# A routed expert's output phase for 96 tokens: from one block of 96 rows to four lanes of 32 rows

## The chip, the cores and the metric

The kernel runs on one core of a Trainium2 chip, in one launch, and all its data is f32. The metric is the device time of that core in microseconds, the median of several runs. Times inside the program come from one profiled execution. A tensor multiplication of f32 stands in the trace as two rows (two weight loads and two matmuls), one for each of its two passes over the same columns.

## The reference, cut to what matters

Two layers are computed for 128 context tokens and 256 latent tokens of width 1024. The change touches only the last part, a SwiGLU with eight experts of which each token uses two:

```
def moe_swiglu(h, w_router, wg, wu, wd):
    t = h.reshape(-1, shp[-1])                     # all 384 tokens
    logits = einsum('td,de->te', t, w_router)
    top_logit, top_e = lax.top_k(logits, 2)
    gates = softmax(top_logit, axis=-1)
    ...                                            # tokens sorted by expert
    def expert_block(args):
        xb, e = args
        return (silu(xb @ wg[e]) * (xb @ wu[e])) @ wd[e]
    ...
    y = zeros_like(t).at[tok_sorted].add(out[dest] * gate_sorted[:, None])
```

`wg` and `wu` are 8 x 1024 x 2816, `wd` is 8 x 2816 x 1024. The 384 tokens give 768 pairs of token and expert.

## The kernel before

Tokens lie on partitions, 128 to a tile, D = 1024 columns. After the attention layer's part the router's result is put into a table (`vtab`) that names a width for each expert: 64, 96, 128, 160, 192, 256 or 384 tokens. `PIECES` splits a width into pieces of 64, 96 or 128 tokens. For the inputs here the experts run as 128+64, 96, 96, 128, 96+64, 96, 64 and 64 tokens (experts 0 to 7), so four pieces have 96 tokens: experts 1, 2 and 5, and the first piece of expert 4.

TensorE has a copy of an expert's code for each of the eight experts and seven widths, and `go_to` branches to the right one by compares (L1044) at the end of the expert before.

An expert's weights come in 33 loads of 1 MB (`MOE_CHUNKS`), issued by SyncE (`moe_load`, L2055) into 11 slots. SyncE issues load n when `moe_used` has reached n - 10, and TensorE raises `moe_used` as it is done with a slot. The last slot of an expert isn't counted (`owed[0] = 0` in `expert`), so 256 increments stand against 264 loads.

An expert has three parts on TensorE:
- **hidden** (L894): for five groups of four 128-wide tiles of the hidden dimension (f tiles 0 to 19), gate and up, tokens as the stationary operand and 512 weight columns moving, over eight k-steps. A piece of 96 tokens is already laid in four lanes of 32 rows of the result: three lanes hold the three token groups of 32 for columns 0 to 383, the fourth holds columns 384 to 511 for each group in turn, side by side. ScalarE does SiLU, VectorE multiplies, and `turn_act` transposes (L939, L943 for 96 tokens).
- **hidden_rest** (L919): the last two f tiles, gate and up in one bank, for 96 tokens as one block of 96 rows and 256 columns. `turn_rest` (L965) transposes them, in the middle of the output part.
- **output** (L992): for 22 f tiles the transposed activations are stationary (128 x tokens) and 512 of the 1024 columns of `wd` move, into two banks. Eleven loads of two f tiles each.

ScalarE and VectorE copy the two banks to `yt`, GpSimd writes them to `expert_out` in DRAM by indirect DMA, one whole-row write for each of the three possible pieces (`y_rows`), and one of half rows (`y_halves`) for the first two, which serves pieces of 64 tokens: `YWRITES = 5` an expert. Row numbers out of bounds are skipped. After expert 7 GpSimd waits for all writes, gathers the rows of each token's later expert, and VectorE adds them to X.

TensorE carries out its own list in order. What else can delay it is a weight load that hasn't landed, or a bank not yet emptied.

## Time and profile before

| | us |
|---|---|
| median of three runs | 2201.76 |
| lowest, highest | 2199.25, 2204.59 |
| the profiled execution | 2182.95 |
| its span, first to last instruction | 2181.0 |
| PE (matmul) busy | 1990.3 |
| PE, weight loads busy | 1282.2 |
| VectorE, ScalarE, GpSimd busy | 445.1, 385.0, 126.8 |
| mean granted TensorE clock | 0.955 of full |

PE busy is the time in which a matmul is under way, several of them counted once. The eight experts take the time from 1190 to 2157 us, 44% of the span; ahead of them are the first layer, attention and the router.

### The profile page before, as it was taken

To read this page: it belongs to the slowest core of one execution; us is meant where nothing else is said; L and a number is where in the kernel's file an instruction comes from. 1 tells how busy PE (TensorE), PEld (TensorE's weight loads), DVE (VectorE), ACT (ScalarE), POOL (GpSimd) and SP (SyncE) were. 2 spreads that over 40 slices of the span, in tenths; PEclk is the share of its full clock that TensorE was granted. 3 is DMA by queue.
4 is the path that set the end of the run, shared out by engine and by line. 5 is a ranking of instruction groups with operands and counts; after the bars stand their busy time and mean duration, and the time that the engine had idled before them with its cause. 6 is when DMAs were issued, how large, how long until landed. Compare 5 with 4: busy or idle time off the path is not lost.

```text
span 2181.0 us, 26973 instructions
## 1 busy us (share of the span) xinstructions
PE 1990.3 (91%) x11623; PEld 1282.2 (59%) x11623; DVE 445.1 (20%) x1078; ACT 385.0 (18%) x819; POOL 126.8 (6%) x104
## 2 busy tenths in 40 slices
PE   4999987799999999987986999999999999998764
PEld 2554547786555578744585554868545774764341
DVE  2440126311000000146423010111011110111032
ACT  2221211302000000243311110212121110122220
POOL 0000123200000000000001000101010100101011
PEclk8999997899999999998897999999999999999998
DMA  9564411022644551221053555899988665899996
GB/s 332 199 228 154 154 60 37 1 78 84 211 168 158 185 163 54 95 69 40 1 178 120 193 193 196 294 342 330 330 282 299 232 215 198 289 335 348 372 386 238
DMA packets 232516, 427.65 MB, mean 196 GB/s; under 512 B 16030, under 2 KB 87165, under 8 KB 232062
## 3 DMA queue, kind: packets, MB, share of 16 engines
q1 hardware_dynamic: 219086, 412.49, 54.1%
q0 software_dynamic: 10208, 12.09, 1.6%
q8 instruction: 111, 1.82, 0.3%
q10 hardware_dynamic: 3088, 1.06, 0.2%
q14 instruction: 23, 0.19, 0.0%
HBM read 427.52 MB, written 25.85 MB: 208 GB/s over the span
## 4 chain that ended last, share of the span: by engine, by line
PE 68%; DMA 7%; DVE 4%; issue 2%; ACT 1%; POOL 0%; SPq 0%; DVEq 0%; POOLq 0%; ACTq 0%
PE bank L894 21%; PE bank L992 13%; PE bank L676 11%; PE bank L497 7%; PE bank L694 5%; PE bank L919 2%; DMA ring<-in_moe_w_gate_dram 2%; DMA ring<-in_moe_w_down_dram 2%; PE bank L435 2%; DMA ring<-in_moe_w_up_dram 1%; PE bank L467 1%; PE bank L766 1%; DMA arena<-in_moe_w_gate_dram 1%; PE bank L765 1%; PE bank L741 1%
## 5 line engine op out<-in xcount | busy, mean ns | idle before, releaser
L894 PE MATMUL bank<-ring,HTXN 128*32 128x128 f32 (+3 forms) x4352 | 410.7, 396 | 45.9 <-issue 18.2
L894 PEld LDWEIGHTS bank<-ring,HTXN 128*32 128x32 f32 (+2 forms) x4352 | 292.6, 122 | 157.0 <-issue 115.5
L1066 ACT ACTIVATE arena<-bank 128x512 f32<-128x512 f32 (+2 forms) x328 | 152.2, 529 | 555.2 <-PE bank L992 197.7
L992 PE MATMUL bank<-ring,arena 128*64 128x512 f32 (+2 forms) x640 | 230.8, 599 | 8.3 <-DMA ring<-in_moe_w_down_dram 8.3
L676 PE MATMUL bank<-HTXN,ring 128*128 128x384 f32 x704 | 231.7, 490 | 2.7 <-DVE HTXN L1412 2.7
L497 PE MATMUL bank<-ring,HTXN 128*128 128x512 f32 (+4 forms) x624 | 196.6, 476 | 3.7 <-DVE HTXN L1412 2.7
L676 PEld LDWEIGHTS bank<-HTXN,ring 128*128 128x128 f32 x704 | 133.6, 191 | 94.8 <-issue 5.5
L1836 DVE TENSOR_TENSOR arena<-arena,bank 128x512 f32<-128x512 f32 x120 | 76.6, 682 | 503.6 <-PE bank L894 503.6
L992 PEld LDWEIGHTS bank<-ring,arena 128*64 128x64 f32 (+2 forms) x640 | 79.6, 157 | 142.7 <-issue 122.0
L497 PEld LDWEIGHTS bank<-ring,HTXN 128*128 128x128 f32 x624 | 114.6, 191 | 81.6 <-issue 71.6
L1340 ACT ACTIVATE arena<-bank 128x512 f32<-128x512 f32 x120 | 65.0, 599 | 404.1 <-PE bank L894 397.3
L694 PE MATMUL bank<-ring,arena 128*128 128x256 f32 x528 | 114.2, 379 | 0.0
L694 PEld LDWEIGHTS bank<-ring,arena 128*128 128x128 f32 x528 | 100.2, 190 | 13.6
L894 PE MATMUL bank<-arena,HTXN 128*32 128x384 f32 (+3 forms) x1088 | 103.6, 393 | 4.3 <-DMA arena<-in_moe_w_up_dram 2.4
L894 PEld LDWEIGHTS bank<-arena,HTXN 128*32 128x32 f32 (+2 forms) x1088 | 72.4, 121 | 31.0 <-issue 19.4
L992 PE MATMUL bank<-arena 128*64 128x512 f32 (+2 forms) x240 | 86.5, 599 | 4.0 <-DMA arena<-in_moe_w_down_dram 4.0
L518 PE MATMUL bank<-HTXN,ring 128*128 128x384 f32 x256 | 83.5, 487 | 1.8 <-DVE HTXN L1412 1.8
L497 PE MATMUL bank<-ring,arena 128*128 128x256 f32 x384 | 83.1, 379 | 1.5 <-DVE arena L1620 1.5
L497 PEld LDWEIGHTS bank<-ring,arena 128*128 128x128 f32 x384 | 72.9, 190 | 11.6 <-issue 1.7
L467 PE MATMUL bank<-ring,sv 128*2 128x512 f32 x384 | 51.0, 653 | 20.6 <-DMA ring<-in_w_mod_dram 20.6
L518 PEld LDWEIGHTS bank<-HTXN,ring 128*128 128x128 f32 x256 | 48.3, 190 | 34.9 <-issue 2.0
L435 PE MATMUL bank<-CST,arena 128*128 128x128 f32 x252 | 42.4, 315 | 26.3 <-DVE arena L1681 14.5
(269 smaller groups left out, 1473.8 us busy)
## 6 DMA issues: line engine op xcount, KB each, us to landing
ring<-in_moe_w_gate_dram SPq DMA_DIRECT2D x64, 1024.0 KB, 6.5
ring<-in_moe_w_up_dram SPq DMA_DIRECT2D x64, 1024.0 KB, 6.6
ring<-in_moe_w_down_dram SPq DMA_DIRECT2D x64, 1024.0 KB, 7.1
ring<-in_w_mod_dram SPq DMA_DIRECT2D x24, 2048.0 KB, 12.2
arena<-in_moe_w_gate_dram SPq DMA_DIRECT2D x24, 1024.0 KB, 7.8
arena<-in_moe_w_up_dram SPq DMA_DIRECT2D x24, 1024.0 KB, 8.2
arena<-in_moe_w_down_dram SPq DMA_DIRECT2D x24, 1024.0 KB, 6.7
ring<-in_w_in_dram SPq DMA_DIRECT2D x10, 2048.0 KB, 9.1
```

What stands on the lines that cost most here:

```text
L435: last = tp(bank[:, k * P:(k + 1) * P], src, ident)
L467: last = mm(bank[q:q + 2, :], sv[:, :, k], w[:, k, :], start=(k < 4), stop=(k >= 4))
L497: last = mm(bank[:, 0:width], lhs[:, k, t * P:(t + 1) * P], w[:, k, :], start=(k == 0), stop=(k == kt - 1))
L518: last = mm(bank[:, 0:TOK], w[:, k, m * P:(m + 1) * P], HT[:, k, :], start=(k == 0), stop=(k == KT - 1))
L676: last = mm(bank[:, 0:TOK], w[:, k, m * P:(m + 1) * P], HT[:, k, :], start=(k == 0), stop=(k == KT - 1))
L694: last = mm(banks[t][0][:, 0:256], aT[:, FH * fh + f, t * P:(t + 1) * P], w[:, f, :], start=(fh == 0 and f == 0), stop=(fh == 1 and f == F ...
L894: last = mm(bank[row:row + rows_, col:col + cn], xe[:, i, k, at:at + rows_], wt[:, c0:c0 + cn], start=(k == 0 and col == 0), stop=(k == KT ...
L919: last = mm(bank[lane * w:(lane + 1) * w, at:at + width], xe[:, i, k, 0:w], wt[:, k, lane * width:(lane + 1) * width], start=(k == 0), sto ...
L992: last = mm(out, act_of(f, i, w), wt[:, f % 2, 512 * h:512 * h + 512], start=(f == 0), stop=(f == FT - 1))
L1066: return act_fn(out, in_, ACT.Copy)
L1340: act_fn(sgm[:, j % 2, i, :], moe_bank_of(("g", j, i))[:, :], ACT.Silu).then_inc(moe_drained(("g", j, i), e)[0], 1)
L1836: v.tensor_tensor(a, a, moe_bank_of(("u", j, i))[:, :], ALU.mult).then_inc(moe_drained(("u", j, i), e)[0], 1)
```

## The change

The output part of a 96-token piece gets the form that the hidden part has. Lanes 0 to 2 (32 tokens each) hold output columns 0 to 767: 512 in the first bank, 256 in the second. The fourth lane holds columns 768 to 1023 of the three token groups in turn, two in the first bank and one in the second. `hidden_rest` is laid out likewise (three lanes of 192 columns and 3 x 64 in the fourth, for gate and for up), and `turn_rest` gathers from it.

In `yt` the last quarter of the rows of tokens 0 to 95 then stands in rows 96 to 127. GpSimd writes the whole rows first (with a last quarter that means nothing), waits for that write to land (`y_whole`), and then issues three writes of quarter rows (`y_quarters`, `write_corner`), which put the right values in place. They are issued for every expert; for a first piece that isn't of 96 tokens their rows are out of bounds. The order of the pieces' writes is reversed. VectorE computes the rows of the corner writes once, in front of the experts.

```diff
-YWRITES = 5
+YWRITES = 7
...
+            v.tensor_scalar(is96, vsum, 1.0, None, ALU.is_equal)
+            for n in range(3):
+                v.tensor_scalar(corner_no[:, 8 * n:8 * n + 8], cnt, lane_row[n], NOROW, ALU.is_le, ALU.mult)
+                last = v.tensor_scalar(corner_f[:, 8 * n:8 * n + 8], base, lane_row[n], 4.0, ALU.add, ALU.mult)
...
+            v.tensor_copy(corner_i, corner_f)
...
                     w = pieces[i][1]
-                    width = 128 * halves(w)
+                    if w == 64:
+                        parts = [(64 * n, 0, 0, 64, 128 * n, 128) for n in range(2)]
+                    elif w == 96:
+                        parts = ([(32 * n, 0, 32 * n, 32, 0, 192) for n in range(3)]
+                                 + [(96, 64 * n, 32 * n, 32, 192, 64) for n in range(3)])
+                    else:
+                        parts = [(0, 0, 0, P, 0, 256)]
...
+                        if w == 96:
+                            tp(bank[:, at:at + w], sgm[0:w, HC % 2, i, 0:P], ident[0:w, 0:w])
+                            tp(bank[0:64, at + w:at + 2 * w], sgm[0:w, HC % 2, i, P:P + 64], ident[0:w, 0:w])
+                            for m in range(3):
+                                last = mm(bank[64:P, at + w + 32 * m:at + w + 32 * m + 32], sgm[w:P, HC % 2, i, 64 * m:64 * m + 64], ident[w:P, w:P],
+                                          start=True, stop=True)
+                            continue
...
+            OUT_96 = ([(0, 32 * n, 0, n, 0, 512) for n in range(3)] + [(0, 96, 0, 0, 768, 256), (0, 96, 256, 1, 768, 256)]
+                      + [(1, 32 * n, 0, n, 512, 256) for n in range(3)] + [(1, 96, 0, 2, 768, 256)])
+
+            def output_96(bank0, bank1, a, wt, f):
+
+                for b, row, col, group, c0, cn in OUT_96:
+                    bank, full = (bank0, bank1)[b]
+                    last = mm(bank[row:row + 32, col:col + cn], a[:, 32 * group:32 * group + 32], wt[:, c0:c0 + cn],
+                              start=(f == 0 and col == 0), stop=(f == FT - 1 and (b == 1 or row < 96 or col > 0)))
+                    if f == 0 and (b, row) == (0, 0):
+                        settle(last)
+                    if f == FT - 1 and row == 96 and (b == 1 or col > 0):
+                        last.then_inc(full, 1)
+                return last
...
+                            if w == 96:
+                                last = output_96(banks[i, 0], banks[i, 1], act_of(f, i, w), wt[:, f % 2, :], f)
+                                continue
...
+                whole = g_.indirect_dma_start(y_rows, at_row(30 + 8 * i + e), yt[:, i, :], None, bounds_check=ROWS - 1, oob_is_err=False)
+                whole.then_inc(y_whole if i == 0 else y_written, 16)
...
+            def write_corner(e, n):
+                g_.indirect_dma_start(y_quarters, at_row(88 + 8 * n + e), yt[:, 0, 256 * n:256 * n + 256], None,
+                                      bounds_check=4 * ROWS - 1, oob_is_err=False).then_inc(y_written, 16)
...
-                for i in range(NPIECE):
+                for i in reversed(range(NPIECE)):
                     write_out(e, i)
+                pool.wait_ge(y_whole, 16 * (e + 1))
+                for n in range(3):
+                    write_corner(e, n)
```

TensorE in the code of a 96-token expert, from `hidden_rest` to the branches at its end, before (rows that repeat are counted behind an x, one for each matmul; the size is weight columns or rows by moving columns):

```order
L919 MATMUL bank<-arena,HTXN 96x256 x16
L939 MATMUL bank<-CST,arena 128x96 x3
L943 MATMUL bank<-CST,arena 128x32 x3
L992 MATMUL bank<-ring,arena 96x512 x8
L965 MATMUL bank<-CST,arena 128x96 x2
L992 MATMUL bank<-ring,arena 96x512 x8
L867 MATMUL bank<-CST,HTXN 128x128 x8
L992 MATMUL bank<-ring,arena 96x512 x16
L992 MATMUL bank<-arena 96x512 x12
L1044 COMPARE_AND_BRANCH x6
```

The same place now, one k-step of `hidden_rest` (there are 16), the turn of it, one f tile of the output part, and the branches:

```order
L932 MATMUL bank<-arena,HTXN 32x192 x3
L932 MATMUL bank<-arena,HTXN 32x64 x3
...
L977 MATMUL bank<-CST,arena 128x96
L978 MATMUL bank<-CST,arena 64x96
L980 MATMUL bank<-CST,arena 64x32 x3
...
L994 MATMUL bank<-arena 32x512 x3
L994 MATMUL bank<-arena 32x256 x6
L1081 COMPARE_AND_BRANCH x6
```

A tile f of the output part was two matmuls of 96 rows and is nine of 32 rows; a k-step of `hidden_rest` for one of gate and up was one and is six.

GpSimd at an expert's end, before:

```order
L1940 DMA expert_out<-arena,idx 768x1024
L1943 DMA expert_out<-arena,idx 1536x512
L1940 DMA expert_out<-arena,idx 768x1024
L1943 DMA expert_out<-arena,idx 1536x512
L1940 DMA expert_out<-arena,idx 768x1024
```

and now, where only the last five stand behind the drain of piece 0:

```order
L1989 DMA expert_out<-arena,idx 768x1024 x2
L1992 DMA expert_out<-arena,idx 1536x512
L1989 DMA expert_out<-arena,idx 768x1024
L1992 DMA expert_out<-arena,idx 1536x512
L1996 DMA expert_out<-arena,idx 3072x256 x3
```

The writes of pieces 2 and 1 went ahead of those of piece 0, and three corner writes came behind.

## Rows read from the trace of the kernel before

**Rows 1.** Stretches: experts 1, 2, 4, 5, 6; busy time, instructions, clock, DMA share.

```profile
core 0: us, PE busy (x) PEld busy (x) DVE busy (x) ACT busy (x) POOL busy (x), PEclk, DMA share, GB/s
...
1375.42:1479.19 103.77, 102.68 (x1121) 75.24 (x1120) 14.26 (x24) 20.29 (x41) 7.96 (x8) 1.00 0.94 333
1479.19:1582.89 103.70, 102.61 (x1122) 75.45 (x1122) 14.27 (x24) 20.29 (x41) 7.96 (x8) 1.00 0.95 332
...
1700.94:1869.50 168.56, 167.69 (x1613) 108.30 (x1612) 14.89 (x24) 21.25 (x41) 7.96 (x8) 1.00 0.60 207
1869.50:1973.28 103.78, 102.69 (x1122) 75.25 (x1121) 14.26 (x24) 20.29 (x41) 7.96 (x8) 1.00 0.94 328
1973.28:2058.13 84.85, 66.36 (x492) 34.22 (x491) 14.86 (x25) 19.70 (x40) 6.98 (x7) 1.00 1.02 376
```

**Rows 2.** Expert 1: L919's min/median/max ns and starts; then in order of time.

```profile
L919 PE MATMUL bank<-arena,HTXN x32: 379/379/457, 1432.6 to 1439.4; 128*96 128x256 f32 x32
...
1439.92 0.37 PE L943 MATMUL bank<-CST,arena 32*128 32x32 f32 x3
1440.21 7.11 PE L992 MATMUL bank<-ring,arena 128*96 128x512 f32 x16
1447.16 0.33 PE L965 MATMUL bank<-CST,arena 96*128 96x96 f32 x2
...
1468.80 10.46 PE L992 MATMUL bank<-arena 128*96 128x512 f32 x24
```

**Rows 3.** 1415.90 to 1426.50, hidden part: the stretch, then groups (busy, mean ns).

```profile
1415.90:1426.50 10.60, 10.60 (x194) 10.42 (x192) 1.88 (x3) 2.46 (x6) 0.00 (x0) 1.00 1.04 402
...
L894 PE MATMUL bank<-ring,HTXN 128*32 128x128 f32 x96 | 10.7, 273 | 0.0
L894 PE MATMUL bank<-ring,HTXN 128*32 128x384 f32 x96 | 10.5, 487 | 0.0
L943 PE MATMUL bank<-CST,arena 32*128 32x32 f32 x2 | 0.3, 222 | 0.0
```

**Rows 4.** Branches ending experts 1, 2, 4, 5, 6: ns min/median/max, starts.

```profile
L1044 PEldq COMPARE_BRANCH  x2: 63/2215/4367, 1471.4 to 1471.5; - x2
...
L1044 PEldq COMPARE_BRANCH  x1: 4618/4618/4618, 1575.2 to 1575.2; - x1
...
L1044 PEldq COMPARE_BRANCH  x2: 75/1706/3337, 1864.0 to 1864.2; - x2
...
L1044 PEldq COMPARE_BRANCH  x3: 63/63/4220, 1965.5 to 1965.7; - x3
...
L1044 PEldq COMPARE_BRANCH  x3: 63/75/6242, 2056.2 to 2056.5; - x3
```

**Rows 5.** Matmuls from expert 1's first compare (1471.40) to 1479.19: busy, mean ns.

```profile
L992 PE MATMUL bank<-arena 128*96 128x512 f32 x19 | 8.3, 592 | 0.0
```

**Rows 6.** Expert 2, hidden part: the sequencer's wait, and its group in time.

```profile
L891 PEldq EVENT_SEMAPHORE  x1: 51/51/51, 1495.8 to 1495.8; - x1
...
1497.05 5.45 PE L894 MATMUL bank<-ring,HTXN 128*32 128x384 f32 x96
```

**Rows 7.** PE in order of time, from expert 6 to expert 7.

```profile
2056.19 1.94 PE L992 MATMUL bank<-arena 128*64 128x512 f32 x8 [0.62 <-DMA arena<-in_moe_w_down_dram]
2062.98 9.23 PE L894 MATMUL bank<-ring,HTXN 128*64 128x256 f32 x64 [4.85 <-issue]
```

**Rows 8.** Stretches behind expert 6's last matmul (columns as in rows 1).

```profile
2058.80:2062.90 4.10, 0.00 (x0) 0.00 (x0) 0.00 (x0) 0.00 (x0) 2.35 (x3) 0.70 1.05 387
2062.90:2066.00 3.10, 3.02 (x15) 1.91 (x17) 0.00 (x0) 0.00 (x0) 2.49 (x3) 0.50 0.83 295
2066.00:2070.00 4.00, 4.00 (x34) 2.77 (x32) 0.00 (x0) 0.62 (x2) 0.08 (x1) 0.84 0.58 170
```

**Rows 9.** Order of time: DVE as expert 0 begins; GpSimd after the last drain.

```profile
1206.07 0.69 DVE L1836 TENSOR_TENSOR arena<-arena,bank 128x512 f32<-128x512 f32 x1 [22.70 <-PE bank L894]
...
2158.84 1.02 POOL L1940 DMA_INDIRECT expert_out<-arena,idx  x1 [79.75 <-ACT arena L1066]
```

35 lines of the change are left out of this document (23 added, 12 removed).

## The prediction

> **What bounds the kernel now.** I read first the stretches of the single experts, then the order of time of TensorE in one 96-token expert, then the branches between experts, and last the two experts at the end. The experts run from 1190 to 2157 of the 2181 us. TensorE is busy in all but 1 us of an expert with a 96-token piece: 102.7 of 103.8 us [rows 1]. There are four such pieces: experts 1, 2 and 5 hold one each (103.8, 103.7 and 103.8 us), expert 4 holds one beside a 64-token piece (168.6 us). In these the time is TensorE's, so matmul time saved there should arrive at the end. Experts 6 and 7 hold 64 tokens each and wait for weights: PE is busy 66.4 of 84.9 us while the DMA engines are full, share 1.02 [rows 1]. The change leaves these two as they are; their transfers are tied to the matmuls ahead of them, so they move forward with the end of expert 5.
>
> In expert 1 the output phase runs from 1440.21 to 1479.19, 39.0 us [rows 2]. A matmul of f32 shows as two rows, one for each pass over its columns.
>
> **Output phase, the gain.** 24 passes of 512 columns with 96-column weights take 10.46 us in all, one of them 0.592 [rows 2, 5]: (10.46 - 0.59)/23 = 0.429 us from one to the next. A tile f has four, 1.716 us. A pass of 256 columns is (1439.4 - 1432.6)/31 = 0.219 us from the next [rows 2]. In the new form lanes 0 to 2 have per f two passes of 512 and two of 256, 2 x (0.429 + 0.219) = 1.30 us; the fourth lane has six of 256, 1.31 us. This holds only if the four lanes run beside each other. The hidden phase of the same piece already has this shape: 96 passes of 384 columns and 96 of 128 in 10.60 us, each kind busy for all of it, so 32 rounds of 0.331 us, in which three lanes do 384 columns and the fourth three times 128 [rows 3]. I take 1.30 us. Saved: 22 x (1.716 - 1.30) = 9.2 us for a piece.
>
> **The last hidden tile pair (L919).** Now 32 passes of 256 columns, 32 x 0.219 = 7.0 us [rows 2]. New: 16 k-steps of two rounds, in a round three lanes of 192 columns and in the fourth three passes of 64. By columns a pass of 64 is 0.056 us (0.110, 0.219 and 0.429 for 128, 256 and 512 lie on 0.83 ns a column and 3 ns), a round 0.168, together 5.4 us. The trace has no round so short. The nearest small passes are the transposes of 32 columns, (0.37 - 0.22)/2 = 0.07 us apart [rows 2, 3]: three are 0.21 a round, 6.7 us. If a round can't be shorter than the 0.331 seen with the same number of instructions [rows 3], it is 10.6 us, a loss of 3.6. I take 5.6, near the columns' value since the lanes of [rows 3] are at it exactly: 1.4 saved, ends +1.6 and -3.6.
>
> **The turn of that pair (L965)** was two transposes, 0.33 us [rows 2]; two remain and three small matmuls of two passes come, 6 x 0.07 = 0.4 us, with a change of array shape: +0.5.
>
> Together 9.2 + 1.4 - 0.5 = 10.1 us a piece, **40.4 us** for four.
>
> **What it loses: the cover of the branches.** At the end of each expert TensorE's instruction stream compares and branches to the next expert's code, and the branch that is taken lasts 3.3 to 6.2 us [rows 4]. Today this costs nothing after experts 0 to 5, since the sequencer is far ahead: expert 1's first compare is at 1471.4, and 19 passes are still to start until 1479.19, 7.8 us of work [rows 4, 5]. The lead is a number of instructions, not a time: in the four-lane hidden phase the sequencer is at the wait ahead of a group at 1495.8, and the group starts at 1497.05, 1.25 us later [rows 6], with again about 18 passes between. In the new output phase 18 passes are one f: 1.30 us. The rest of the branch is then bare. What it looks like is seen once, after expert 6: 8 passes in two lanes (1.94 us) stand ahead of a branch of 6.24 us, and PE is idle for 4.85 [rows 7].
>
> A compare that falls through costs 0.13 us, and from a branch's end to the first matmul it is 0.27 (2056.5 + 6.24 against 2062.98). Stalls: after expert 1, 0.13 + 4.37 + 0.27 - 1.30 = 3.5; after 2, 4.62 + 0.27 - 1.30 = 3.6; after 4 (its 96-token piece is the last of a pair), 0.13 + 3.34 + 0.27 - 1.30 = 2.4; after 5, 0.25 + 4.22 + 0.27 - 1.30 = 3.4. Sum 12.9. The branch is short where the DMA share is 0.60 (3.34), 4.2 to 4.6 at 0.94, 6.24 at 1.02 [rows 1, 4]; the shorter output phase drives the share of experts 1, 2 and 5 up, so I add 0.6 to each: **14.7**. After experts 0, 3, 6 and 7 nothing changes.
>
> The clock comes on top. In the stall after expert 6 the granted clock fell from 1.00 (2.4 GHz) [rows 1] to a mean of 0.70 while the engine stood, was 0.50 (1.2 GHz) in the next 3.1 us and 0.84 in the 4 after that [rows 8]: 1.55 + 0.64 = 2.2 us of matmul time. I charge it to the three stalls of over 3 us and 1.0 to the short one: **7.6**. From below this is 0: the 1.1 us for which PE is idle in experts 1, 2 and 5 leave the clock at 1.00 [rows 1].
>
> The Trainium skill (TensorE: Matmul & The Clock Gate, its table of specifications) gives TensorE's queue a depth of 64. The 19 passes of [rows 5] and as many weight loads are about 38 entries, so this trace doesn't bear 64 out. With 64 entries the lead would be 32 passes, 2.3 us, each stall 1.0 shorter, and the sum 4 us better.
>
> **Other engines.** GpSimd issues seven writes an expert for five. One keeps it busy for 1.0 us [rows 9], and it has nothing else for tens of us between experts; the wait of the corner writes holds only them and the next gather, a whole expert ahead of its use. At the very end five writes follow the last drain one by one from 2158.84 [rows 9]. The three of the empty pieces now go ahead of that drain and three corner writes follow it, again five; the wait for the whole write to land is at least partly under the half write: 0 to +1, I take 0.3. The 12 new small DVE operations fall into 22.7 us in which DVE is idle [rows 9], where even 1 us each would fit: 0. What they hold back is the index table that GpSimd needs only at the end of expert 0. The added write traffic, at most 96 KB an expert, is a tenth of one of the 33 loads: 0.
>
> **Sum.** -40.4 + 14.7 + 7.6 + 0.3 = **-18 us**. The profiled execution (2182.95 us, span 2181.0) would take 2165; the timed runs stand 0.9% above it, and I put the same 18 us against their median of 2201.76: **2184 us**.
>
> **The rivals.**
> *The branches stay covered* (the lead is longer than I read, or the fetch runs on while lanes drain). Then the full gain comes, less DMA limits. With the DMA engines full expert 6 gets through its 33 loads in 84.9 us [rows 1], and the new expert needs 93.7: the DMA engines are near, but not the bound. 2201.8 - 40 = 2162, or 2166 with small losses. Against it speaks the wait position in [rows 6]. Chance 0.18.
>
> *The last hidden pair becomes bound by its instructions.* Its round has six passes and six weight loads in 0.168 us, twice as dense as anything in the trace. If a round stays at 0.331 us, the pair costs 10.6 instead of 5.6 us, 20 us over four pieces; with branches at their upper end (6.24 us each and 2.2 for every clock drop, 7 us more) the kernel is at -18 + 20 + 7 = +9, 2211 us. Alone it gives 2204, no change. It turns the sign from 10.1 us a piece on. Chance 0.10, of which 0.06 slower.
>
> The Trainium skill (TensorE: Matmul & The Clock Gate, Wait — 56ns, not 53.3ns?) has such a rule: with hardware decode off the sequencer spends about 62 ns on each MATMUL, the bound once the array work is shorter. By it a pair's 192 passes would be 11.9 us and the kernel at about 2209. The six passes in 0.331 us of [rows 3], 55 ns each, already beat it, so I leave it at the chance above.
>
> *The four lanes of the output phase don't overlap*, the fourth runs behind the three: 2.6 us an f for 1.72, +78 us, 2280. [rows 3] speak against it. 0.02, slower.
>
> *The transfers take the gain.* Expert 5 loads the first weights of expert 6. If the DMA engines can't keep up in its shortened phase, its 10 us of gain are waited out again in expert 6: -18 + 7 = -11, 2191. Today they run at a share of 0.94 through experts 1, 2 and 5 [rows 1]. Chance 0.15.
>
> **How the numbers follow.** My forecast, gain with bare branches, has 0.55: from -10 (all branches 6.24 us, every clock drop) to -27 (no clock loss, short branches). Full gain 0.18, transfers 0.15, bound pair 0.10, serial lanes 0.02. The range reaches from 2160 to 2196 and leaves out the serial lanes, the bound pair and the tails. A difference under 0.2% (4.4 us) is about what a measurement of this kernel can't tell from none. Faster 0.87, same 0.05, slower 0.08.
>
> **What the profile after would show.** Output phase of expert 1 at 29 to 30.5 us for 39.0, 11 steps of 2.6 us. The pair at 5.4 to 6.7 us. At the ends of experts 1, 2, 4 and 5 PE idle by "issue", 2 to 5 us each, and the clock at 0.5 behind them; the expert stretches at 97 to 100 us for 103.8. Wrong would be: no such idle time (then 2162), or steps over 3 us, or waits for down weights in expert 5.

## The result, and the profile after

| | before | after |
|---|---|---|
| median, us (4 runs each) | 2201.98 | 2181.64 |
| lowest, highest | 2199.25, 2204.59 | 2177.39, 2183.98 |
| profiled execution, its span | 2182.95, 2181.0 | 2181.5, 2179.7 |

The ratio after to before is 0.9906, with a 95% interval of 0.9886 to 0.9925: 20 us faster, where the forecast was 18. One thing has to be said at once. The two profiled executions differ by 1.5 us only: the trace of before was taken 19 us under that kernel's timed median, the trace of after at its median. So the 20 us can't be found by laying these two traces side by side. What can be compared in them are single steps, and the experiments supply the rest. (This section's trace is called the first changed trace below.)

The stretches of experts 1, 2, 4, 5 and 6 in the changed kernel, cut as in [rows 1] from the first hidden matmul of an expert to that of the next (columns as there):

```profile
1374.93:1476.36 101.43, 95.13 (x1596) 79.45 (x1597) 14.97 (x25) 20.29 (x41) 13.11 (x14) 1.00 0.97 347
1476.36:1582.33 105.97, 96.42 (x1595) 81.82 (x1595) 14.27 (x24) 20.30 (x41) 10.91 (x11) 0.97 0.91 326
...
1702.19:1865.14 162.95, 159.00 (x2089) 111.00 (x2093) 15.60 (x25) 21.26 (x41) 11.51 (x12) 1.00 0.63 216
1865.14:1967.98 102.84, 96.45 (x1596) 81.96 (x1597) 14.28 (x24) 20.29 (x41) 12.24 (x13) 0.98 0.95 337
1967.98:2058.46 90.48, 68.93 (x493) 36.61 (x495) 14.18 (x24) 20.29 (x41) 9.90 (x10) 0.96 1.00 368
```

PE busy fell from 102.7 to 95 or 96 us in a 96-token expert, but the stretches fell by only 2.3 and 0.9 us (experts 1 and 5), and that of expert 2 grew by 2.3. Experts 1 to 5 together take 593.0 us here, from 1374.9 to 1968.0, where before took 597.9. In [rows 1] PE was busy in all but 1 us of such a stretch. Now 6 to 10 us are idle.

Expert 1 from its output part on, in order of time (PE):

```profile
1440.35 5.39 PE L994 MATMUL bank<-ring,arena 128*32 128x512 f32 x72
1445.66 0.30 PE L977 MATMUL bank<-CST,arena 96*128 96x96 f32 x1
...
1446.44 5.39 PE L994 MATMUL bank<-ring,arena 128*32 128x512 f32 x72
1451.76 1.09 PE L874 MATMUL bank<-CST,HTXN 128*128 128x128 f32 x8
...
1463.95 7.93 PE L994 MATMUL bank<-arena 128*32 128x512 f32 x105
1476.28 0.81 PE L901 MATMUL bank<-ring,HTXN 128*32 128x384 f32 x3 [4.40 <-issue]
1479.52 3.21 PE L901 MATMUL bank<-ring,HTXN 128*32 128x384 f32 x24 [2.44 <-issue]
```

72 passes are four f tiles. The second such group takes from 1446.44 to 1451.76, 5.32 us, 1.33 us an f tile, against 1.716 in [rows 2]. The turn takes from 1445.66 to 1446.44, 0.78 us. The output part ends at 1471.9, 31.5 us after it began, where [rows 2] had 39.0. Then PE waits 4.40 us for nothing that the profile shows, starts three passes, and waits another 2.44.

What the sequencer does there is seen in its branches. These are the ones that end experts 1, 2, 4 and 5 (nanoseconds min/median/max, and their starts; the longest is the one that is taken), to be held against [rows 4]:

```profile
L1081 PEldq COMPARE_BRANCH  x2: 63/3110/6157, 1469.7 to 1469.8; - x2
...
L1081 PEldq COMPARE_BRANCH  x1: 6273/6273/6273, 1575.7 to 1575.7; - x1
...
L1081 PEldq COMPARE_BRANCH  x2: 75/1941/3807, 1860.8 to 1861.0; - x2
...
L1081 PEldq COMPARE_BRANCH  x3: 63/63/6122, 1961.3 to 1961.5; - x3
```

The branch behind expert 1 starts at 1469.80, and 1469.80 + 6.16 = 1475.96 is 0.32 us ahead of the matmul at 1476.28. Its lead is 1471.9 - 1469.8 = 2.1 us. The matmuls that are under way or still to start at that moment:

```profile
L994 PE MATMUL bank<-arena 128*32 128x256 f32 (+1 forms) x29 | 2.6, 431 | 0.0
```

So 29 passes by the same reading that gave 19 in [rows 5], but worth 2.1 us for 7.8.

The clock and the transfers around that gap (columns as in [rows 1]):

```profile
1471.90:1476.30 4.40, 0.02 (x2) 0.05 (x3) 0.69 (x1) 0.18 (x1) 1.94 (x2) 1.00 1.01 375
1476.30:1480.00 3.70, 1.26 (x9) 0.49 (x13) 0.00 (x0) 0.00 (x0) 0.49 (x1) 0.61 0.15 51
1480.00:1484.00 4.00, 4.00 (x44) 3.42 (x43) 0.00 (x0) 0.00 (x0) 2.44 (x3) 0.51 0.09 22
1484.00:1488.00 4.00, 4.00 (x81) 4.00 (x75) 0.00 (x0) 0.60 (x1) 0.00 (x0) 1.00 0.54 168
```

TensorE restarts at half its clock (1.2 GHz: the granted clock is 0.61 in the stretch that still has the second wait in it, and 0.51 in the next), and 44 matmuls take the place of the 81 of a later stretch of the same length. The DMA engines are full while TensorE stands, and nearly idle (0.15 and 0.09) as it starts again: the slots are filled and none is given back. This looked like a second loss, and is tested below.

### The profile page after: what moved, and what is told of

Read it like the earlier page. It is cut to its first block, busy times and chain, and to the rows that moved or that the text cites. A ratio compares the mean times of both kernels' runs of the same rounds, so it can differ in the third digit from the quotient of the medians.

```text
span 2179.7 us, 30827 instructions
## 1 busy us (share of the span) xinstructions
PE 1965.0 (90%) x13519; PEld 1304.5 (60%) x13519; DVE 448.2 (21%) x1092; ACT 384.7 (18%) x819; POOL 150.3 (7%) x128
## 4 chain that ended last, share of the span: by engine, by line
PE 67%; DMA 6%; DVE 4%; issue 3%; ACT 1%; POOL 0%; SPq 0%; ACTq 0%; DVEq 0%; POOLq 0%
PE bank L901 21%; PE bank L683 10%; PE bank L504 7%; PE bank L1029 6%; PE bank L994 5%; PE bank L701 5%; PE bank L932 2%; DMA ring<-in_moe_w_down_dram 2%; DMA ring<-in_moe_w_gate_dram 2%; PE bank L442 1%; DMA arena<-in_moe_w_gate_dram 1%; PE bank L474 1%; PE bank L773 1%; PE bank L772 1%; PE bank L737 1%
## 5 line engine op out<-in xcount | busy, mean ns | idle before, releaser
L901 PE MATMUL bank<-ring,HTXN 128*32 128x128 f32 (+3 forms) x4352 | 423.7, 403 | 66.0 <-issue 40.0
L901 PEld LDWEIGHTS bank<-ring,HTXN 128*32 128x32 f32 (+2 forms) x4352 | 299.0, 124 | 182.1 <-issue 138.9
L1029 PE MATMUL bank<-ring,arena 128*64 128x512 f32 (+1 forms) x384 | 118.2, 602 | 8.6 <-DMA ring<-in_moe_w_down_dram 8.6
L701 PEld LDWEIGHTS bank<-ring,arena 128*128 128x128 f32 x528 | 100.2, 190 | 13.6
L901 PE MATMUL bank<-arena,HTXN 128*32 128x384 f32 (+3 forms) x1088 | 105.3, 398 | 2.6 <-DMA arena<-in_moe_w_up_dram 1.4
L994 PE MATMUL bank<-ring,arena 128*32 128x256 f32 (+1 forms) x1152 | 88.3, 452 | 0.7 <-issue 0.4
L1029 PEld LDWEIGHTS bank<-ring,arena 128*64 128x64 f32 (+1 forms) x384 | 39.1, 154 | 76.2 <-issue 56.2
L994 PEld LDWEIGHTS bank<-ring,arena 128*32 128x32 f32 x1152 | 49.2, 110 | 38.0 <-issue 9.0
```

The lines of the kernel that those rows point to most:

```text
L701: last = mm(banks[t][0][:, 0:256], aT[:, FH * fh + f, t * P:(t + 1) * P], w[:, f, :], start=(fh == 0 and f == 0), stop=(fh == 1 and f == F ...
L901: last = mm(bank[row:row + rows_, col:col + cn], xe[:, i, k, at:at + rows_], wt[:, c0:c0 + cn], start=(k == 0 and col == 0), stop=(k == KT ...
L994: last = mm(bank[row:row + 32, col:col + cn], a[:, 32 * group:32 * group + 32], wt[:, c0:c0 + cn], start=(f == 0 and col == 0), stop=(f == ...
L1029: last = mm(out, act_of(f, i, w), wt[:, f % 2, 512 * h:512 * h + 512], start=(f == 0), stop=(f == FT - 1))
```

## Experiment 1: both kernels again, and both without branches

Four kernels on one chip. `before_again` and `after_again` are the two kernels as they are. The other two have no compares and no branches between experts: the code for this input's widths stands in one line. The edit is the same in both:

```diff
-            pe.br("experts")
...
-                    expert(e, PIECES[v])
-                    go_to(e + 1, body_of(e, v))
...
+            for e, v in enumerate([4, 1, 1, 2, 3, 1, 0, 0]):
+                if e > 0:
+                    for q in range(2):
+                        pe.wait_ge(*moe_drained(("X", 0, q), e - 1))
+                expert(e, PIECES[v])
```

> The kernel before, unchanged, run again with a profile. Its first profiled execution took 2182.95 us, its timed executions 2199 to 2205, so the trace on which the forecast rests may be of an untypically fast execution. If that is so, this execution takes about 2200 us, and its trace shows in which stretch the missing 19 us are. If they lie in the eight experts, the base of my sum was too low and the trace-to-trace difference (before 2181.0, after 2179.7) says nothing of the change; if they lie ahead of the experts, the change is worth little and the timed gain of 20 us is for another reason.

> The changed kernel, unchanged, run again beside the kernel before on the same chip: 2178 to 2184 us, 0.99 of it. The stalls behind experts 1, 2, 4 and 5 come back in this trace, 2.5 to 5 us each, as in its first trace (4.4, 4.8, 2.5, 4.5). If they are an accident of one execution they move or vanish.

> The kernel before, but with the eight experts' code for this input's widths written one behind the other, with no compares and branches (it would be wrong for other inputs). Theory of the bare branch: in the kernel before only the branch at the entry and the one behind expert 6 are bare (3.3 and 4.9 us idle and about 2 us for the clock each), and expert 6 and 7 wait for weights anyway: 5 to 10 us faster than before. Rival (branches cost nothing, the time between experts is the weights'): no difference.

> The changed kernel without compares and branches in the same way. Theory of the bare branch: the stalls behind experts 1, 2, 4 and 5 (16 us of idle PE in the trace, 2.4 more as the stream restarts, and about 8 us of half clock) go too, so it is 25 to 30 us faster than the changed kernel, less what the weight loads then hold back, and 35 to 40 us faster than the straight form of the kernel before. Rival (the transfers take the gain): it gains at most 10 us on the changed kernel, and PE waits for weights in experts 2 and 5.

Measured, against 2184.11 us for the kernel before on this chip (17 runs):

| | median, us | ratio to before, 95% interval |
|---|---|---|
| before_again | 2182.14 | 0.9988, 0.9977 to 0.9999 |
| after_again | 2175.05 | 0.9960, 0.9943 to 0.9976 |
| straight_before | 2175.76 | 0.9964, 0.9950 to 0.9978 |
| straight_after | 2140.20 | 0.9792, 0.9775 to 0.9808 |

`before_again` is the same kernel as the 17 runs, and yet reads 2 us less, with an interval that just leaves out 1. Differences of 2 us or so between two sets of runs therefore mean nothing here, and the intervals are somewhat too narrow.

Two things follow. **The base was off.** The first of the four expectations had asked for about 2200 us; on this chip the kernel before takes 2184 us, and the change is worth 9 us (7 against `before_again`) for 20. The two intervals, 0.9886 to 0.9925 and 0.9943 to 0.9976, don't meet. In the later experiments, on two more chips, the kernel before took 2183 and 2182 us.

**The branches take most of the gain.** Without them the change is worth 2175.76 - 2140.20 = 35.6 us; with them 9. The same edit gives 8 us to the kernel before and 35 to the changed one, where 25 to 30 was expected. The stretches of experts 1 and 2, in `after_again` and then in `straight_after`:

```profile
1379.47:1478.49 99.02, 93.09 (x1596) 79.79 (x1589) 14.85 (x25) 20.30 (x41) 13.01 (x14) 1.00 0.98 356
1478.49:1583.76 105.27, 96.62 (x1595) 81.47 (x1593) 14.27 (x24) 20.30 (x41) 10.93 (x11) 0.97 0.92 328
```

```profile
1370.84:1465.89 95.05, 93.27 (x1595) 80.22 (x1598) 14.26 (x24) 19.73 (x41) 11.40 (x12) 1.00 0.98 350
1465.89:1561.43 95.54, 93.04 (x1602) 80.07 (x1594) 14.26 (x24) 20.47 (x42) 10.93 (x11) 1.00 1.02 364
```

All eight experts of the four traces, cut in the same way, in us:

| expert | before_again | straight_before | after_again | straight_after |
|---|---|---|---|---|
| 0 | 186.0 | 185.3 | 186.0 | 186.4 |
| 1 | 103.8 | 103.8 | 99.0 | 95.1 |
| 2 | 103.7 | 103.7 | 105.3 | 95.5 |
| 3 | 118.1 | 118.1 | 119.8 | 118.2 |
| 4 | 168.6 | 168.6 | 161.5 | 158.3 |
| 5 | 103.8 | 103.8 | 100.2 | 95.4 |
| 6 | 89.5 | 85.7 | 89.7 | 85.4 |
| 7 | 94.7 | 96.4 | 94.5 | 95.8 |

In the kernel before the branches cost nothing in experts 1 to 5. What its straight form gains is the branch ahead of expert 0 (PE idle by "issue" for 13.1 us there, and for 9.2 without it) and the one behind expert 6 (3.8 us); expert 7 gives 1.7 of it back. In the changed kernel experts 1 to 5 lose 4.0, 9.8, 1.6, 3.2 and 4.8 us to them, 23.4 in all. Expert 2's share is so large because it holds the restart behind expert 1 and its own branch at the end. The loss of expert 3 goes with the restart behind expert 2, since its own branch is covered. The sum is not the same in every execution: experts 1 to 5 take 585.8 us in `after_again` and 593.0 in the first changed trace, against 562.5 in `straight_after`, so there it is 30.5 us.

Between `before_again` and `after_again` experts 1 to 5 gain 12.1 us, but the spans of the traces differ by only 2.9. The rest lies ahead of the experts: they begin at 1186 us in the one and 1193 in the other. Over all fourteen traces of this case that beginning lies between 1183 and 1193 us, with a median of 1190 both in the four of the kernel before and its edited forms that branch and in the seven of changed kernels with branches. It differs between executions, not between the kernels, and a comparison of two single traces has to go by their stretches.

Free of branches, a 96-token expert takes 95.1 to 95.5 us. The prediction's sum was 103.8 - 10.1 = 93.7. `straight_after` shows its parts:

```profile
1427.93 5.62 PE L932 MATMUL bank<-arena,HTXN 128*32 128x192 f32 x192
1433.49 0.47 PE L952 MATMUL bank<-CST,arena 96*128 96x96 f32 x3
...
1434.18 1.91 PE L994 MATMUL bank<-ring,arena 128*32 128x512 f32 x19
1436.78 4.09 PE L994 MATMUL bank<-ring,arena 128*32 128x512 f32 x53 [0.69 <-issue]
...
1441.57 5.39 PE L994 MATMUL bank<-ring,arena 128*32 128x512 f32 x72
1446.89 1.09 PE L874 MATMUL bank<-CST,HTXN 128*128 128x128 f32 x8
```

The pair takes 1433.49 - 1427.93 = 5.56 us, as forecast. Behind it PE waits 0.69 us in the middle of plain code, with no branch near. That instructions come late there too is shown under experiment 2.

## Experiment 2: each half of the change alone

Two kernels on a second chip, where before took 2183.28 us (15 runs). `only_output` has the new output part and writes, with the old `hidden_rest` and turn:

```diff
-                        parts = ([(32 * n, 0, 32 * n, 32, 0, 192) for n in range(3)]
-                                 + [(96, 64 * n, 32 * n, 32, 192, 64) for n in range(3)])
+                        parts = [(0, 0, 0, 96, 0, 256)]
```

`only_rest` is the other half:

```diff
-                            if w == 96:
-                                last = output_96(banks[i, 0], banks[i, 1], act_of(f, i, w), wt[:, f % 2, :], f)
-                                continue
...
-                pool.wait_ge(y_whole, 16 * (e + 1))
-                for n in range(3):
-                    write_corner(e, n)
```

> The changed kernel with hidden_rest and turn_rest of a 96-token piece as before; output part in four lanes, three more writes. Theory (bare branches behind the output part): the output part carries nearly the whole change. Gain of four pieces 4 x 22 x (1.716 - 1.33) = 34 us, bare branches and the clock behind them unchanged against the changed kernel (about 27 us), so some 7 us under the kernel before and 3 to 5 us over the changed one (4 x (7.0 - 5.9) + the 1.17 us gaps at L932). Stretch of expert 1 about 1.1 us longer than in the changed kernel. Rival (the short rounds of hidden_rest are what makes the sequencer late at the end of the piece): the idle time by issue behind experts 1, 2 and 5 falls to under 1 us and the kernel is 15 us faster than the changed one.

> The changed kernel with the output part and its writes as before (five writes an expert, the order of the pieces' writes stays reversed); hidden_rest and turn_rest in four lanes. Theory: the branch behind an output part of 96x512 passes is covered again (7.8 us of lead), so no idle time by issue behind experts 1, 2, 4 and 5, and the gain is that of the pair alone: 4 x (7.0 - 5.9 - 0.3) = 3 us, up to 5, less 1 for gaps: 2 to 5 us under the kernel before, PE idle by issue in all about 10 to 15 us. Rival (the longer code or its place in memory makes the branches bare): idle time by issue stays at 30 us or more and the kernel is 15 us or more slower than before.

Measured: `only_output` 2174.23 us, ratio 0.9960 (0.9946 to 0.9974); `only_rest` 2179.58, ratio 0.9983 (0.9971 to 0.9994). The output part alone gives what the whole change gives (0.9960 of before in both, on two chips); it was expected to be 3 to 5 us slower than the whole. The new `hidden_rest` and turn add nothing that can be measured, though their own time is lower where nothing interrupts it: 6.98 us and 0.31 in `only_output`, 5.56 and 0.77 in `straight_after`, 1.0 us a piece.

`only_rest` tells what makes a branch bare. Expert 2's branch in it, and the matmuls around it:

```profile
L1078 PEldq COMPARE_BRANCH  x1: 4573/4573/4573, 1582.8 to 1582.8; - x1
```

```profile
1580.17 10.46 PE L1026 MATMUL bank<-arena 128*96 128x512 f32 x24
1590.47 1.88 PE L901 MATMUL bank<-ring,HTXN 128*128 128x512 f32 x4
```

With 96x512 passes ahead of it again, the branch of 4.57 us is covered and PE doesn't stop. So the short passes of the output part are what uncovers it, and not the longer code of `hidden_rest`, which `only_rest` has. That the longer code of the output part plays a part is not excluded by this kernel alone, but the lead above (29 passes worth 2.1 us) needs no further cause. In this profiled execution (the longest of the ten of `only_rest`) there is however a new wait of 2.13 us in the middle of expert 1's `hidden_rest`:

```profile
1442.76 2.21 PE L932 MATMUL bank<-arena,HTXN 128*32 128x192 f32 x47 [2.13 <-issue]
```

`after_again` has one of 1.41 us at the same line in expert 2, and the first changed trace one of 1.17. A wait of that size in one or two of the four pieces eats half of the pair's gain (4 us) or more.

Why was the bare branch 6.2 us and not 4.4? The first place to look is the transfers during the branch itself (DMA share and GB/s are the last two columns). First `before_again` at the ends of experts 1, 2 and 6, then the changed kernel at the ends of experts 1, 2 and 4:

```profile
1468.15:1472.50 4.35, 4.35 (x11) 1.63 (x10) 0.00 (x0) 0.00 (x0) 0.00 (x0) 1.00 0.97 324
1571.80:1576.34 4.54, 4.54 (x12) 1.68 (x11) 0.00 (x0) 0.00 (x0) 0.00 (x0) 1.00 0.96 320
...
2052.87:2059.15 6.28, 1.44 (x8) 0.27 (x4) 0.00 (x0) 0.60 (x1) 2.42 (x3) 0.90 1.05 387
```

```profile
1469.80:1475.96 6.16, 2.08 (x29) 1.13 (x21) 0.69 (x1) 0.60 (x1) 1.94 (x2) 1.00 1.04 383
1575.70:1581.97 6.27, 1.80 (x28) 1.09 (x19) 0.69 (x1) 0.60 (x1) 1.94 (x2) 1.00 1.03 381
...
1861.00:1864.81 3.81, 1.56 (x26) 0.64 (x15) 0.69 (x1) 0.60 (x1) 2.24 (x3) 1.00 0.55 202
```

At 381 to 387 GB/s a taken branch lasts 6.2 or 6.3 us, at 320 to 324 it lasts 4.4 or 4.5, at 202 it lasts 3.8. As a rule this mean over the branch fails: in `after_again` the branch behind expert 5 takes 6.63 us at 329 GB/s and in `after_chain` (below) 6.22 at 331, while covered branches behind expert 3 take 4.0 to 4.3 us at 336 to 346; `only_output` has one of 7.52 us at 316 behind expert 3 and one of 4.88 at 92 ahead of expert 0. Instruction code does come over these engines: between 1468 and 1484 us the changed kernel's trace has this queue beside the weights'.

```profile
q1 hardware_dynamic: 1516, 3.00, 50.8%
q0 software_dynamic: 368, 0.35, 6.5%
q8 instruction: 4, 0.07, 1.8%
```

The single packets of that queue, whose own times stand in the packed traces, say more. The eleven traces with branches have 93 taken ones, and each holds a packet of 16 KB of instructions whose end is followed by the end of the branch 0.9 to 1.6 us later (median 1.4). The packet itself takes 0.9 to 1.7 us, and no longer where the engines are full (1.0 to 1.3). For which engine a packet is the trace doesn't tell; that one comes at the same place in every branch is the evidence. What varies is the wait until it starts, and that goes with the transfers just ahead of the branch. Two microseconds ahead of the branch behind expert 1, in `before_again` and in the first changed trace (columns as above):

```profile
1465.93:1467.93 2.00, 2.00 (x6) 0.79 (x5) 0.00 (x0) 0.00 (x0) 0.00 (x0) 1.00 0.86 261
```

```profile
1467.85:1469.85 2.00, 2.00 (x34) 1.42 (x30) 0.00 (x0) 0.00 (x0) 0.00 (x0) 1.00 1.05 383
```

The packet starts 1.9 us behind the start of the branch in the first and 3.7 in the second. Over all 93: where hardly anything is moved until it starts (under 60 GB/s, 37 branches), it starts after 0.9 to 1.5 us and the branch takes 3.3 to 4.1; where the engines are busy during that wait but moved 214 to 306 GB/s in the two microseconds ahead of the branch (31), after 1.2 to 2.2 us, and the branch takes 3.8 to 4.6, but for the 7.52 us of `only_output` (5.0 us, at 269 GB/s ahead); where they moved 347 to 407 ahead of it (24), after 3.6 to 4.1 us, and the branch takes 6.0 to 6.7. The last one is the 4.88 us ahead of expert 0 in `only_output` (2.5 us, nothing moved ahead of it). So the longer branch is shown to be a longer wait for its code's transfer to start, and it goes with engines that are already full as the branch begins. Why they are full is argued: the output part in lanes gives slots back faster, and the transfers behind it start sooner. No kernel was run with the transfers taken away, and the two outliers stay open.

The waits in plain code have the same mark. The changed kernels and `only_rest` have 17 waits by "issue" of 0.6 to 2.8 us in `hidden_rest` and the output part of experts 1 to 5, the 0.69, 1.17, 1.41 and 2.13 us above among them, and each ends 1.2 to 1.6 us behind the end of a 16 KB packet of instructions. So does the second wait behind expert 1's branch, 2.44 us in the first changed trace (1.2 us behind another such packet).

## Experiment 3: is it the branch, or the transfers that it lets run dry?

Two kernels on the chip of experiment 2. `after_chain` lays TensorE's code out by width: behind expert e for a width stands expert e+1 for the same width, and six compares to the other widths fall through to it. For these inputs experts 1 to 2 and 6 to 7 then go on without a taken branch.

```diff
-            for e in range(NE):
-                for v in ORDER:
+            for v in ORDER:
+                for e in range(NE):
...
-                    go_to(e + 1, body_of(e, v))
...
+                    others = [n for n in ORDER if n != v]
+                    for n, other in enumerate(others):
+                        nxt = body_of(e + 1, v) if n + 1 == len(others) else f"{body_of(e, v)}_not{n + 1}"
+                        pe.br_eq(variant[e + 1], other, on_true=body_of(e + 1, other), on_false=nxt)
```

`after_depth` counts the last slot of each expert in `moe_used`, so that SyncE issues each load eleven slots ahead throughout (before: one slot fewer with every expert):

```diff
+                    owed[0] = int(e > 0)
                     expert(e, PIECES[v])
```

> The changed kernel, in which the last slot of each expert is counted too (owed[0] starts at 1 behind expert 0), so that SyncE issues each load as early in expert 7 as in expert 0 (eleven slots ahead; now eight at expert 3, four at expert 7). Theory (the branch is long, 6.1 to 6.3 us, and its cover is a matter of instructions alone): the branches stay bare, PE idle by issue stays near 37 us; what shrinks is only the wait for weights, by less than 3 us, since a load that comes earlier doesn't make the DMA engines faster. Rival (part of the 9 to 20 us that are missing is lost because the DMA engines run dry in the stalls of later experts and experts 6 and 7 then wait for it): more depth gives back 5 to 12 us in experts 5 to 7. A third outcome: more transfers beside the branches make these longer, and the kernel slower by up to 5 us.

> The changed kernel with TensorE's code laid out by width instead of by expert: behind the code of expert e for a width stands that of expert e+1 for the same width, and six compares to the other widths fall through to it. For these inputs only experts 1 to 2 (96 and 96 tokens) and 6 to 7 (64 and 64) go on without a taken branch; behind 0, 2, 3, 4, 5 and 7 a branch is taken as now. Theory (the bare time is the fetch of code behind a taken branch): the idle time by issue at 1476 (4.40 and 2.44 us) and at 2058 (4.93 us) goes, with 2 us of clock each: 8 to 14 us under the changed kernel, less what experts 6 and 7 wait for weights anyway (5 us), so 5 to 10. Rival (the bare time is that of the compares or of the wait on the semaphore of the emptied bank): both stay and the time doesn't move.

Measured: `after_chain` 2160.81 us, ratio 0.9894 (0.9875 to 0.9912); `after_depth` 2159.16, ratio 0.9889 (0.9870 to 0.9907). Each is some 15 us under the changed kernel's ratio of 0.9960.

`after_chain`, expert 1 into expert 2, in order of time:

```profile
1462.28 7.99 PE L994 MATMUL bank<-arena 128*32 128x512 f32 x108
1470.02 10.73 PE L901 MATMUL bank<-ring,HTXN 128*32 128x384 f32 x192
```

No wait, no slow restart: the 192 passes take 10.73 us. Expert 1 takes 93.7 us (the prediction's sum to a tenth, but 94.8 to 96.0 in the three other traces without a branch behind it, two of which have waits in its plain code) and expert 2, which still ends in a bare branch, 99.9 for 105.3. The six compares cost nothing that shows. So the bare time is the fetch behind a taken branch, and its rival (compares, or the wait for the emptied bank) falls. Both kernels gained more than was expected: 14 us for 5 to 10 from the layout, 16 from the depth where the theory had under 3 and its rival 5 to 12. Of the layout's gain experts 1 to 5 give 10.9 us (574.9 for the 585.8 of `after_again`) and expert 6 gives 3.0.

The gain of `after_depth` spoke for the other suspicion: that the DMA engines' idle time at the restarts is waited out in experts 6 and 7. But that can only be said once the same edit was made to the kernel before.

## Experiment 4: the same edits in the kernel before, and both together

Four kernels on a third chip, where before took 2181.58 us (7 runs). The edits are those of experiment 3 and, in the last kernel, that of experiment 1.

> The kernel before, with the last slot of each expert counted too (the one-line edit that took 16 us off the changed kernel). Theory (the depth is worth the same to both, since experts 6 and 7 wait for weights in both: 89.5 and 94.7 us now, 73.6 and 93.2 in the changed kernel with depth): experts 6 and 7 fall to about 75 and 93 us and the kernel gains 15 us, 2168; against it the changed kernel with depth (2159) is then 9 us faster, as without depth. Rival (the depth gives back what the stalls of the changed kernel cost the DMA engines, which the kernel before doesn't have): it gains under 5 us, and the change is worth 20 us or more once the depth is there.

> The kernel before with the depth and with TensorE's code laid out by width, so that no branch is taken from expert 1 to 2 and from 6 to 7. The branch behind expert 1 is covered there, so only the 4.9 us ahead of expert 7 and the clock behind them (2.2) can go: 4 to 7 us under the kernel before with depth alone, since with the depth experts 6 and 7 wait less for weights. Rival (experts 6 and 7 are still bound by transfers): no difference from before_depth.

> The changed kernel with both edits. Alone the layout took 14 us and the depth 16 us off. If the two savings are of different things (one of bare branches, the other of experts 6 and 7 waiting for weights) they add: 2145 us. If they overlap in experts 6 and 7 (the layout's 4 us there, and the DMA engines as the next bound), 2150 to 2155. Against before_chain_depth: 10 to 16 us faster, since one of the four bare branches is gone.

> The changed kernel without compares and branches (TensorE's code for this input's widths in one line) and with the depth. The bound of what the branches still cost: without depth the straight form is at 2140. If experts 6 and 7 can use the weights that come earlier, 2140 - 10 to 16 = 2124 to 2130; if they are at the rate of the DMA engines already, 2138. From 2145 or so for after_chain_depth the rest is the three bare branches behind experts 2, 4 and 5 with their clock, about 15 us.

| | median, us | ratio to before, 95% interval |
|---|---|---|
| before_depth | 2166.56 | 0.9927, 0.9911 to 0.9944 |
| before_chain_depth | 2164.69 | 0.9918, 0.9902 to 0.9935 |
| after_chain_depth | 2146.53 | 0.9828, 0.9812 to 0.9845 |
| straight_after_depth | 2127.76 | 0.9746, 0.9723 to 0.9769 |

The depth gives the kernel before 15 us, as much as it gave the changed one. Expert 6 in `before_depth` and in `after_depth`:

```profile
1973.34:2047.81 74.47, 63.40 (x492) 33.78 (x491) 14.87 (x25) 20.29 (x41) 9.36 (x10) 1.00 1.03 380
```

```profile
1965.36:2038.95 73.59, 64.75 (x493) 35.46 (x493) 14.18 (x24) 20.29 (x41) 9.91 (x10) 0.96 1.02 377
```

Both fall from 89.5 us to about 74. With depth in both, the change is worth 0.9889 / 0.9927 = 0.996, the same as without, though the two were measured on two chips. The layout adds only 2 us to the kernel before (4 to 7 expected), no more than noise: expert 6 falls from 74.5 to 71.4 us with its branch gone, but expert 7 waits longer for weights, 95.6 us for 91.9. The idle DMA engines at 1476 to 1484 us looked like a loss and are none of the change's: the transfers had only run ahead as far as the slots allow.

`after_chain_depth` is the version that beats both: 35 us (1.7%) under the kernel before. The two savings (14 and 16) nearly add: 0.9960 less 0.9828 is 29 us. With both edits on either side the change is worth 2164.69 - 2146.53 = 18 us instead of 9 (10 to 16 expected). The edits were made for their mechanism, but the code still serves any input; how often the layout saves a branch depends on how often neighbouring experts have the same width. The remaining three bare branches and the one ahead of expert 0 still cost 2146.53 - 2127.76 = 19 us.

## The tail

GpSimd at the end of `after_again`, in order of time:

```profile
2150.84 0.96 POOL L1989 DMA_INDIRECT expert_out<-arena,idx  x1 [18.55 <-ACT arena L1103]
2152.11 0.98 POOL L1992 DMA_INDIRECT expert_out<-arena,idx  x1 [0.30 <-issue]
2155.18 0.98 POOL L1996 DMA_INDIRECT expert_out<-arena,idx  x1 [2.10 <-DMA expert_out<-arena,idx]
2156.46 0.98 POOL L1996 DMA_INDIRECT expert_out<-arena,idx  x1 [0.30 <-issue]
2157.74 0.98 POOL L1996 DMA_INDIRECT expert_out<-arena,idx  x1 [0.30 <-issue]
2160.59 1.05 POOL L1983 DMA_INDIRECT arena<-expert_out,idx  x1 [1.87 <-DMA expert_out<-arena,idx]
```

Behind the two writes stands a wait of 2.10 us for the whole write, then the three corner writes. From the end of TensorE's last matmul to the end of the span it is 2177.6 - 2153.9 = 23.7 us in `before_again`, 2174.7 - 2149.3 = 25.4 in `after_again`, and 2183.4 - 2163.3 = 20.1 in `only_rest`, which has the reversed order of the writes without the corners. By these the reversed order gives 3.6 us and the corners take 5.3: 1.7 net, where the prediction had 0.3. In the other traces the kernel before and its forms have 23.4 to 23.7 us, and the changed kernels 23.9 to 25.4, so the net lies between 0.3 and 1.8. Of what `only_rest` gained (3.7 us in the medians, of which 2 are within the noise) the order of the writes would explain all by itself. A kernel without the last corner writes was not run.

## Why the prediction was right, and where it was not

**The mechanism held.** The forecast was a gain from shorter matmuls of which more than half is taken back by branches that lose their cover, with stalls by "issue" behind experts 1, 2, 4 and 5 and the clock at 0.5 behind them. All of it is in the trace, and it is shown, not only argued, by taking the branches away (35.6 us against 9), by covering them again (`only_rest`), and by removing one (`after_chain`). The part ahead of the prediction names two things that can delay TensorE, a weight load that hasn't landed and a bank not yet emptied. The runs show a third, instructions that haven't come.

**The gain, 40.4 us forecast, 35.5 measured** (experts 1 to 5 of `straight_before` less those of `straight_after`; the medians, which have the tail in them, give 35.6). An f tile takes 1.33 us for the 1.30 of the sum: 22 x 0.03 x 4 = 2.6 us. The turn takes 0.46 us more than before (0.5 forecast), and the pair 5.56 (5.6 forecast). That leaves 2.3 us, and the waits by "issue" inside the pieces, which the sum didn't have, are 3.5 us (2.8 at L932 and the 0.69 above in `straight_after`): they cover it, with 1.2 us over. The prediction was at "The trace has no round so short": it sought the cost of many short passes in the round's length, and it came in single late fetches instead.

**The branches and the clock, 14.7 + 7.6 = 22.3 us forecast, 23.3 measured** (the difference of `after_again` and `straight_after` in experts 1 to 5). That these are so near is luck: in the first changed trace it is 30.5, and in `after_again` the parts are off against each other. The four stalls are 4.83, 4.81, 2.82 and 5.41 us, 17.9 for 14.7, and a second wait of 1.34 comes behind the first. Plain code has 1.9 us less of waits in it than `straight_after`, and some 6 us are left for the clock, for 7.6. Behind expert 4 (2.82 us idle) the granted clock stays at 1.00 in this trace, and is 0.65 in the mean of the 4 us behind the stall in the first changed one (2.49 us idle). The lead is not 18 passes or 1.30 us but 2.1 us (29 passes, of which some are already under way in the four lanes), 0.8 us more cover each. And the branches behind experts 1, 2 and 5 last 6.1 to 6.6 us and not 4.2 to 4.6 plus 0.6. The prediction saw the direction (share up, branch longer) and named 6.24 us as the upper end; it was passed. Its measure, the DMA share of the whole expert (0.94 before, 0.91 to 0.97 after), hardly moved; what moved was the transfer rate just ahead of the branch, 228 to 261 GB/s before and 349 to 407 after. The idle times in the first changed trace came at 4.40, 4.75, 2.49 and 4.48 us for 4.1, 4.2, 2.4 and 4.0. The second wait at a restart (2.44 us behind expert 1, 1.34 in `after_again`, none in `only_output`) was not foreseen.

On the lead, the Trainium skill (TensorE: Matmul & The Clock Gate, its table of specifications) gives TensorE's queue 64 entries. The prediction set that aside for the 38 of [rows 5]. In the new output part the 29 passes and the weight loads still to come (21 in the row of the branch under experiment 2, 29 at most) are 50 to 58 entries, nearer to the page's figure, and the 2.3 us that the prediction worked out from it were the better estimate of the lead; why it is 38 or fewer with 96x512 passes no run here shows.

**The rival of the pair bound by its instructions** fell: 192 passes in 5.56 us are 0.029 us a pass. The Trainium skill (same page, Wait — 56ns, not 53.3ns?) has 62 ns for each MATMUL with hardware decode off, which would have made 11.9 us of it. The trace shows no such bound in four lanes; whether hardware decode is on here, which by the page would lift it, no run shows.

**The rival of the transfers** fell as well, as stated: experts 6 and 7 take 184.2 us in `before_again` and in `after_again`, so none of the gain is waited out there (186.6 for 184.1 in the first pair of traces). Experiment 4 shows the same from the other side.

**The tail, 0.3 us forecast, 1.7 measured (0.3 to 1.8 over all traces).** The step "again five" counted the writes and took the wait ahead of the corners as partly hidden; it is 2.10 us and bare. The small VectorE operations are 14 and not 12; they cost nothing that shows, since the experts begin no later.

**The base, and luck.** The forecast was 2184 us, from 2202 down by 18, and the result 2182. In the three experiment sessions, each on another chip, the kernel before stood at 2182 to 2184; the changed kernel was run in the first of them, and was 7 to 9 us faster. With the terms as measured there the sum is -35.5 + 23.3 + 1.7 = -10.5, and by the first pair of traces only -4.9 + 1.6 = -3.3. So the mechanism accounts for 3 to 11 us of gain and not for the 20 of the first measurement: that the forecast of -18 came so near to it is luck. It was 9 too good for what the later runs show. The hint was on the table: the profiled execution of before was at 2182.95, below all three timed runs, and the prediction noted the 0.9% without asking what it was. Why the kernel before took 19 us more in those timed runs stays open; no trace of such a run exists.

The steps announced for the profile after: output part of expert 1 at 29 to 30.5 us (31.5 measured), pair at 5.4 to 6.7 (5.56 to 5.95 where nothing interrupts it for long), idle 2 to 5 us by "issue" (2.5 to 5.4), stretches at 97 to 100 (99.0, 105.3 and 100.2 in `after_again`; expert 2 pays for the restart and for its own branch).

## What to carry to other kernels

In this kernel branches between code bodies are free as long as the instructions queued ahead of them last longer than the fetch. Whoever shortens instructions without reducing their number shortens that cover: multiply the queued instructions by their new duration and compare it with the taken branch, measured where the DMA engines are already full as it begins. Dense short instructions can also wait for their code where no branch is. And try an edit that helps the changed kernel on the old one too before its gain is credited to the change's cause.

## What the runs showed of the hardware that was not expected

- A taken branch of TensorE's sequencer lasted 3.3 to 4.1 us where nearly nothing was moved as it began (37 branches), 3.8 to 4.6 where the core's transfers ran at 214 to 306 GB/s in the 2 us ahead of it (30, and one of 7.5), and 6.0 to 6.7 at 347 to 407 (24). Each held one 16 KB packet of instructions that ended 0.9 to 1.6 us ahead of its end; only the wait until that packet started grew. A compare that fell through took 63 to 75 ns, and six of them cost nothing that shows.
- Four lanes of 32 columns take a pass every 0.029 us (192 in 5.56 us, 192 and 64 columns mixed), but instructions then run out at times: waits of 0.6 to 2.8 us in code without a branch near, each 1.2 to 1.6 us behind the end of a 16 KB packet of instructions.
- Behind a bare branch came a second wait of 1.3 to 2.4 us after three passes in three of the traces (the first changed one, `after_again`, `after_depth`), and none in `only_output`.
- A stall of 2.8 us left TensorE's granted clock at 1.00 behind expert 4 in `after_again`, and behind one of 2.5 us in the first changed trace its mean over the next 4 us was 0.65.
- The median of one and the same kernel was 2202 us in the first measurement and 2184, 2183 and 2182 on the three chips of the experiments.
